# Prompt attention: the score products of the two softmax maps issued in turn on the two halves of the array's rows, small steps in alternating banks

## What is computed

```python
def diff_attn_core(q, k, v, qpos, kpos, rel_bias, lam):
    k2 = k.reshape(B, Tk, H_DIFF, 2, QK_HEAD_DIM)
    s = jnp.einsum('bqhmd,bkhmd->bhmqk', q, k2).astype(jnp.float32) * (QK_HEAD_DIM ** -0.5)
    ...
    s = jnp.where(dist >= 0, s + bias[None, :, None], NEG_INF)
    p = jax.nn.softmax(s, axis=-1)
    a = p[:, :, 0] - lam * p[:, :, 1]
    return jnp.einsum('bhqk,bkhd->bqhd', a.astype(v.dtype), v)
```

## Time and profile before

| what | value |
|---|---|
| median of three runs | 1637.46 us (1637.44 to 1640.38) |
| span of the profiled execution | 1635.5 us |
| TensorE busy, share of the span | 95% |
| share of TensorE in the chain that ended last | 91% |
| prompt attention, steps in order | from 291.0 us to about 477 us |
| time of one whole head at full clock | 41.27 us |

### The profile page before, as it was taken

How to read it: one execution, slowest core, us unless ns; L and a number is a source line. 1 busy time by engine, 2 the same in 40 slices (tenths; PEclk the granted TensorE clock), 3 DMA queues, 4 the chain that set the end, 5 groups by cost and what they waited for, 6 DMA issues and landing times.

```text
span 1635.5 us, 21501 instructions
## 1 busy us (share of the span) xinstructions
PE 1561.5 (95%) x8338; PEld 1320.6 (81%) x8338; DVE 716.4 (44%) x1041; ACT 450.2 (28%) x731; POOL 165.0 (10%) x313
## 2 busy tenths in 40 slices
PE   6999999999988999899999999999999999999993
PEld 5999999566655445488898989999898989999883
DVE  5234221455552211334456354554546354554547
ACT  4421020345541111222342313132232323132231
POOL 1161000011110000011200000000000000000007
PEclk9999999589999999899999999999999999999997
DMA  6101221120007674132220101010110101010106
GB/s 225 53 27 55 71 77 42 34 84 1 1 21 210 203 250 142 49 131 84 84 77 27 58 19 64 20 65 18 64 51 26 64 13 64 26 64 13 39 27 202
DMA packets 94149, 116.26 MB, mean 71 GB/s; under 512 B 6524, under 2 KB 65317, under 8 KB 94085
## 3 DMA queue, kind: packets, MB, share of 16 engines
q1 hardware_dynamic: 92277, 112.25, 21.6%
q10 hardware_dynamic: 1760, 3.01, 0.5%
q0 software_dynamic: 48, 0.13, 0.0%
HBM read 100.69 MB, written 14.69 MB: 71 GB/s over the span
## 4 chain that ended last, share of the span: by engine, by line
PE 91%; DVE 3%; POOL 2%; ACT 2%; SPq 1%; DMA 1%; issue 1%; POOLq 0%; ACTq 0%; DVEq 0%
PE PS L1803 32%; PE PS L1840 16%; PE PS L1546 15%; PE PS L1781 6%; PE PS L1600 5%; PE PS L1699 3%; PE PS L1671 3%; PE PS L1604 2%; PE PS L1625 2%; PE PS L1658 2%; PE PS L1615 1%; POOL y_acc L1080 1%; DVE wo_lo L1358 1%; PE PS L1682 1%; PE PS L1534 0%
## 5 line engine op out<-in xcount | busy, mean ns | idle before, releaser
L1803 PE MATMUL PS<-act_hi,wu_hi 128*128 128x364 f32 x1056 | 347.7, 329 | 3.6 <-DVE wu_lo L1370 2.6
L1803 PE MATMUL PS<-act_lo,wu_hi 128*128 128x364 f32 x1056 | 347.7, 329 | 0.0
L1803 PE MATMUL PS<-act_hi,wu_lo 128*128 128x364 f32 x1056 | 347.5, 329 | 0.0
L1803 PEld LDWEIGHTS PS<-act_hi,wu_hi 128*128 128x128 f32 x1056 | 199.1, 189 | 4.3 <-DVE wu_lo L1370 2.7
L1803 PEld LDWEIGHTS PS<-act_lo,wu_hi 128*128 128x128 f32 x1056 | 199.1, 189 | 0.4
L1803 PEld LDWEIGHTS PS<-act_hi,wu_lo 128*128 128x128 f32 x1056 | 199.1, 189 | 0.0
L1412 DVE TENSOR_TENSOR y_acc<-y_acc,PS 128x512 f32<-128x512 f32 (+1 forms) x198 | 135.1, 685 | 140.2 <-PE PS L1840 138.3
L1840 PE MATMUL PS<-wd_hi,g_hi 128*128 128x512 f32 x360 | 143.5, 399 | 0.0
L1840 PE MATMUL PS<-wd_lo,g_hi 128*128 128x512 f32 x360 | 142.7, 396 | 0.0
L1840 PE MATMUL PS<-wd_hi,g_lo 128*128 128x512 f32 x360 | 142.6, 396 | 0.0
L968 ACT CAST g_hi<-conv 128x1088 fp32r<-128x1088 f32 x22 | 24.3, 1104 | 275.8 <-PE PS L1840 219.8
(11 more groups left out here) (227 smaller groups left out, 2538.2 us busy)
## 6 DMA issues: line engine op xcount, KB each, us to landing
wu_raw<-in_w_up_dram SPq DMA_DIRECT2D x44, 512.0 KB, 3.8
kpage<-in_cache_k_dram SPq DMA_DIRECT2D x64, 256.0 KB, 3.0
vpage<-in_cache_v_dram SPq DMA_DIRECT2D x64, 256.0 KB, 2.9
wd_raw<-in_w_down_dram SPq DMA_DIRECT2D x22, 512.0 KB, 5.3
w_raw<-in_w_in_dram SPq DMA_DIRECT2D x20, 512.0 KB, 4.7
x_in<-in_x_prompt_dram SPq DMA_DIRECT2D x8, 512.0 KB, 5.8
wo_raw<-in_w_out_dram SPq DMA_DIRECT2D x8, 512.0 KB, 5.2
x_res<-in_x_prompt_dram SPq DMA_DIRECT2D x8, 512.0 KB, 4.3
```

Of the source, the lines that this page charges most:

```text
L1803: mm = nc.tensor.matmul(PS[:, 3 * half + c, 0:CW], a[:, half, k, :], b[:, k, CHUNKS[c]], start=(j == 0), stop=(j == len(parts) - 1))
```

## The change

`scores(i)` now does both maps. It first issues the products with the keys for both maps in turn, chunk by chunk, and then the bias products of map 0 (raising `score_ready`) and of map 1. A new function `score_cols` gives the banks: a step of at most 512 columns uses one bank for each map, the first or second of its pair by turns, so that steps n = 2, 3 and 4 wait for the softmax of the step two back; all others (n = 1 and n = 5 to 8) wait for `prob_ready` of both maps of the step just before.

```diff
--- before.py
+++ after.py
@@ -440,6 +440,12 @@
 
     def turns_before(i):
         return sum(turns(j) for j in range(i))
+
+    def score_cols(i, m):
+
+        w = P * (i % QB + 1)
+        bank = 2 * m + (i % 2 if w <= 512 else 0)
+        return PS[:, bank:bank + (w + 511) // 512, :].rearrange("p a b -> p (a b)")[:, 0:w]
 
     sbias_loaded = sem("sbias_loaded")
     sbias_zero = sem("sbias_zero")
@@ -813,8 +819,7 @@
             if i >= 2:
                 act.wait_ge(turn_ready, turns_before(i - 1))
             w = P * (i % QB + 1)
-            src = PS[:, 2 * m:2 * m + 2, :].rearrange("p a b -> p (a b)")[:, 0:w]
-            nc.scalar.activation(prob[:, i % 2, m, 0:w], src, ACT.Exp, bias=nmax[:, i % 4, m:m + 1],
+            nc.scalar.activation(prob[:, i % 2, m, 0:w], score_cols(i, m), ACT.Exp, bias=nmax[:, i % 4, m:m + 1],
                                  accum_out=prob_sum[:, i % 4, m:m + 1]).then_inc(prob_ready, 1)
 
         def out_square(i):
@@ -1213,8 +1218,7 @@
 
         def row_max(i, m):
             dve.wait_ge(score_ready, 2 * i + m + 1)
-            src = PS[:, 2 * m:2 * m + 2, :].rearrange("p a b -> p (a b)")[:, 0:P * (i % QB + 1)]
-            nc.vector.tensor_reduce(nmax[:, i % 4, m:m + 1], src, AX.X, ALU.max, negate=True).then_inc(nmax_ready, 1)
+            nc.vector.tensor_reduce(nmax[:, i % 4, m:m + 1], score_cols(i, m), AX.X, ALU.max, negate=True).then_inc(nmax_ready, 1)
 
         def mix(i):
 
@@ -1583,26 +1587,31 @@
         for q in took[-8:]:
             pe.wait_ge(*q)
 
-        def scores(i, m):
+        def scores(i):
             h, n = i // QB, i % QB + 1
             w = P * n
             if i == 0:
                 pe.wait_ge(bias_lo_ready, 1)
-            if i >= 1:
-                pe.wait_ge(prob_ready, 2 * (i - 1) + m + 1)
-            d = slice(DH * m, DH * m + DH)
+            last_user = i - 2 if 1 <= i % QB <= 3 else i - 1
+            if last_user >= 0:
+                pe.wait_ge(prob_ready, 2 * last_user + 2)
             qs = slice(NS + P * (n - 1), NS + P * n)
+            b0 = max(0, w - 2 * P)
             for c in range(0, w, 512):
                 e = min(c + 512, w)
-                out = PS[:, 2 * m + c // 512, :]
-
-                b0 = max(c, w - 2 * P)
-                mm = nc.tensor.matmul(out[:, 0:e - c], qT[d, h, qs], kT[d, h, NS + c:NS + e], start=True, stop=b0 >= e)
-                if b0 < e:
-                    t = slice(b0 - (w - 2 * P), e - (w - 2 * P))
-                    for j, b in enumerate((bias_hi, bias_lo)):
-                        mm = nc.tensor.matmul(out[:, b0 - c:e - c], identr[:], b[:, h, t], start=False, stop=(j == 1))
-            mm.then_inc(score_ready, 1)
+                biased = max(c, b0)
+                for m in range(2):
+                    d = slice(DH * m, DH * m + DH)
+                    nc.tensor.matmul(score_cols(i, m)[:, c:e], qT[d, h, qs], kT[d, h, NS + c:NS + e], start=True, stop=biased >= e)
+            for m in range(2):
+                for c in range(0, w, 512):
+                    e = min(c + 512, w)
+                    biased = max(c, b0)
+                    if biased < e:
+                        t = slice(biased - (w - 2 * P), e - (w - 2 * P))
+                        for j, b in enumerate((bias_hi, bias_lo)):
+                            mm = nc.tensor.matmul(score_cols(i, m)[:, biased:e], identr[:], b[:, h, t], start=False, stop=(j == 1))
+                mm.then_inc(score_ready, 1)
 
         def turn(i):
             n = i % QB + 1
@@ -1636,11 +1645,9 @@
 
         for i in range(NSTEP + 4):
             if i < NSTEP:
-                scores(i, 0)
+                scores(i)
             if 0 <= i - 2 < NSTEP:
                 weigh(i - 2)
-            if i < NSTEP:
-                scores(i, 1)
             if 0 <= i - 1 < NSTEP:
                 turn(i - 1)
             if i >= OB + 3 and (i - OB - 3) % OB == 0:
```

## The result

The changed kernel takes 1645.74 us (median of 13 runs) where the kernel before takes 1639.77 (13 runs): ratio 1.0036, 95% interval 1.0026 to 1.0046. It is slower by about 6 us.

What follows compares the result with a forecast made beforehand. The prediction took TensorE's own work to bound the stage. 1637.5 us, plus 18.2 for the loop in three heads, minus 1 for the first head, plus 9 for the clock, gave 1663.7, rounded to 1663 us; range 1648 to 1702.

Steps and rivals of the forecast that it cites:

- What bounds the stage: Prompt attention before the change: bound by TensorE's own work, busy 39.9 of 41.2 us in a head.
- the loop: Steps n = 5 to 8: closed chain through TensorE, VectorE and ScalarE between steps' scores, 8.54 us at n = 8; +6.05 us per head.
- the overlap term: Score passes of both maps on the array's two halves: partial overlap, saving 4.8 us of TensorE work per head.
- 5 pass lengths for 8, at one chunk 3 for 4: Score passes of both maps: eight passes take five pass lengths at n = 8, four take three at one chunk.
- if passes start in order: Passes on the two halves: assumed to start in order, one at a time per half, giving 5 pass lengths for 8.
- The small steps: n = 1 to 4 of a full-clock head: taken as 0, bounds -1.9 and about +1.9 us.
- The first head: First head of the prompt attention, at the lower clock: estimated -1 us, bounds -4 and +5.
- the full clock coming back to this head: Rival for the first head: both halves at work keep the clock up, 14.3 us won; chance 0.1 with its second condition.
- a second condition: In that rival: small steps at their best bound, 3 x -1.9 us, had to hold too.
- not slower: Rival: first head gets its full clock back and small steps are at their best, 1636 us; chance 0.1.
- the first head ran at the lower clock: First head before the change: clock fell from 2.4 to 1.2 GHz for some 44 us, with TensorE busy throughout.
- The later clock: Three later heads: one clock fall of 6 to 10 us each, 3 us a head, +9 us; bounds 0 and +60.

Runs made afterwards that it cites:

- e1: Changed kernel with VectorE's, ScalarE's and TensorE's orders moved so nothing of the step before stands in the loop; 1611.12 us, ratio 0.9832 to the kernel before.
- e6: Changed kernel with key products issued as map 0's two chunks, then map 1's; 1644.96 us, ratio 1.0026 to the kernel before.
- e3: Changed kernel with idle 128-row products in TensorE's two gaps at n = 5 to 8; 1637.2 us, ratio 0.9992 to the kernel before.
- e7: Changed kernel without the alternating banks, so every step waits for both exponentials of the step just before; 1659.64 us, ratio 1.0128 to the kernel before.
- e9: Kernel before with 8 idle products in each of the first three steps, run once more for a second profile; 1617.83 us, ratio 0.9862.
- e4: Kernel before with 8 idle products behind the scores of each of the first three steps; 1618.19 us, ratio 0.9872.
- e2: Kernel before, maps still apart, with the same moved orders as e1; 1648.0 us, ratio 1.0058.
- e5: Changed kernel with keys and bias of map 0, then of map 1; 1683.82 us, ratio 1.0256 to the kernel before; second profile's run 1688.68 us.
- e13: e5 with 12 idle products in the gap ahead of the key products at n = 5 to 8; 1649.76 us, ratio 1.007 to the kernel before.
- e11: Kernel before with key products over all 128 rows, both maps getting the sum of both maps' scores; 1602.35 us, ratio 0.9773.
- e12: Kernel before with each map's queries in a tile whose other 64 rows are zero, so key products run over 128 rows; 1605.78 us, ratio 0.9799.
- e14: e5 with key products over all 128 rows, both maps getting the sum of both maps' scores; 1629.51 us, ratio 0.9943 to the kernel before.
- e8: e1 with out_norm of the step four back, ahead of or between VectorE's maxima; 1612.48 us, ratio 0.9829 to the kernel before.

## Why the prediction was wrong

**What bounds the stage, and the loop: right.** The loop of n = 5 to 8 is there, at 8.08 us for n = 8 against 8.54; apart from the overlap term its pieces are within 0.04 us. TensorE's busy time at full clock fell and the stage did not follow. e1 shows it by opening the loop: -35 us against the changed kernel, of which the loop has some 28. The direction, slower, was right.

**The overlap term: too small.** "5 pass lengths for 8, at one chunk 3 for 4" was wrong; it is 4 for 8. The step that failed here is "if passes start in order". In e6 four passes of map 0 are issued ahead of map 1's first, and the bias still starts after 1.93 us. The Trainium skill says in "TensorE: Matmul & The Clock Gate", section "Part 3: Packing small matmuls — row/col tiling", that products on different row groups run concurrently, and the 1.92 us here agree. The Trainium skill also says there that they start and end in program order; the 1.93 us of e6 speak against that, for fp32 products of two passes. The bias of n = 8 was to start 2.3 us after the first key pass with overlap and 3.6 without; it started after 1.92. The overlap that was mis-sized made each loop 0.46 to 0.57 us too long in the forecast: 30.2 us for n = 5 to 8 against 28.2, +6.05 against +4.1 a head. Over three heads that is 6 us.

**The small steps: taken as 0, measured -0.75 us a head** (16.4 against 17.12 in e3), inside the bounds. Without the alternating banks they would have cost (e7).

**The first head: the term that failed most.** The forecast was -1 us, "bounds -4 and +5"; it was -10.3. I had the right mechanism as a rival, the full clock coming back to this head for up to 14.3 us, but gave it 0.1 and coupled it to a second condition, so that it stood for "not slower" and not for a term of the sum. The step that failed is "the first head ran at the lower clock", carried over to the changed kernel without a reason. In the changed kernel this head is at the low clock for 13.7 us, from about 301 to 315, instead of 44. e9 shows what the clock had cost that head before: at least 17.8 us, more than the 14.3 I had reckoned from the other heads. Why the clock came back so early in the changed kernel stays open (below).

**The later clock: about right in size.** Forecast +9 us in three heads; against the full-clock head of e3 it was 5.9 + 1.0 + 0.9 = 7.8 us. The dips of the later heads lasted 3.4 to 7 us.

With the measured terms the sum is 3 x 3.3 - 10.3 + 7.8 = +7 us, with 6 measured between medians and 9.5 between the profiled spans. Of the 19 us between that sum and the forecast's +26 (18.2 - 1 + 9), the first head has 9, the overlap 6, the small steps 2 and the later clock 1. All of them missed to the same side.

**Slips in the forecast's own arithmetic.** 1663.7 was rounded down to 1663. The savings listed for the overlap add up to 4.9 us a head, not 4.8. And with the first head at -4 and the small steps at -1.9 three times, the lower bound without a fall of the clock is 1637.5 + 18.2 - 4 - 5.7 = 1646, not 1648. The measured 1645.74 us lies just below that too, with a first head of -10.3 where the bounds were -4 and +5.

**What I had not asked** is why the clock stayed low for 44 us in a first head in which TensorE never paused. With the halves one after the other, the longest fall was 44 us before, 48 in e4's odd profile, 58 in e2, 34 and 44 in e5's two profiles and 24 in e13, but 7 in e9, whose heads ran the same key products at full clock for 170 us. So half-array products go with a low clock that stays low; they don't make it fall each time. With the whole array (e11, e12, e14) the longest fall was 14 us. With both halves side by side it was at most 14 us in five kernels (changed, e1, e3, e6, e8), but 31 us in e7, which waits for `prob` in every step.

What is shown is that e5's kernel with whole-array passes (e14) and the kernel before with them (e12) lose the long falls. Whether it is the rows at work or the pauses at the block changes isn't separated: whole-array passes remove both. That the two halves side by side help too is argued from e5 against the changed kernel, which differ in TensorE's work as well (2.5 us a head by e13), and e7 speaks against a simple rule; this stays open. Of e11's 37 us the first head has 21.5 (55.6 to 34.1), mostly clock, and the full-clock heads show 4.3 us each of the block changes.

## What to carry to other kernels

An engine that is 95% busy can have its work cut and the stage still get slower, if the cut puts the other engines' work in a row behind it. Add up the loop through all engines first, from one product to the next use of its banks, and move everything that belongs to another step out of it. Then the lighter work of the engine pays, as e1 shows (37.7 us a head against 41.3). And before trusting a stage's time, read the clock over it: a head 14 us longer than its likes was here a larger prize than the edit. It was won by 24 idle products in eight of nine executions, or by padding a 64-row product to 128 rows, which here cost TensorE no time and saved each change between the two.

## What the runs showed of the hardware

- Eight fp32 passes of 512 columns on 64 rows, four on each half, took 1.92 us with the change to 128-row products at their end, as four did before (1.91), and 1.93 with all of one half issued first (e6).
- A pass of 512 columns takes 0.43 us on 64 rows (from 1.91 and 1.48 us in the earlier trace rows) and on 128 (1.72 us for four in e11). A block of 64-row products between 128-row ones costs about 0.4 us more: 1.91 and 0.44 us for scores and bias against 1.72 and 0.24 in e11.
- The granted clock fell to half (2.4 to 1.2 GHz) and stayed there for 44 us with TensorE busy throughout, its key products on half of the array. In the same program with whole-array key products (e11), and with 24 idle whole-array products at the start (e9), it held through that stretch.
